# The experts' stationary operands woven: high and low words in turn, 128 bytes away from the moving weights

## The reference

```
probs / top 2 of 8 experts for each token
for an expert x:   gu = tokens_x @ w_gu[x]          # 1024 -> 2 * 2816
                   h  = silu(gu[:, :2816]) * gu[:, 2816:]
                   y  = h @ w_down[x]               # 2816 -> 1024
token = layer_norm(alpha * token + gate * y ...)
```

## Time and profile before

| what | value |
|---|---|
| median of three runs | 1770.74 us |
| the profiled execution, its own time | 1766.83 us |
| its span in the trace | 1765.0 us |
| TensorE matmul busy | 1743.4 us, 99% of the span |
| VectorE busy | 1361.9 us, 77% |
| ScalarE busy | 1076.1 us, 61% |
| granted TensorE clock, mean | 0.996 of full speed |
| DMA, mean over the span | 254 GB/s |

### The profile page before, as it was taken

The page is one execution under the profiler, slowest core; times in us unless marked ns, Lnnn a source line. Parts: engine busy times, 40 slices in busy tenths (PEclk is TensorE's granted clock), DMA queues, the critical chain, the costliest instruction groups (busy, mean ns, idle before and its releaser), DMA issues.

```text
span 1765.0 us, 26513 instructions
## 1 busy us (share of the span) xinstructions
PE 1743.4 (99%) x11249; PEld 1571.6 (89%) x11249; DVE 1361.9 (77%) x1591; ACT 1076.1 (61%) x1200; POOL 157.7 (9%) x165
## 2 busy tenths in 40 slices
PE   9999999999999999999999999999999999999997
PEld 8999999999988999998998888888888888888885
DVE  6895488677764667656687899888889898889897
ACT  7654455565644454443446777777777777767674
POOL 1454170000000100000030100000000000000110
PEclk9999999999999999999999999999999999999999
DMA  9332364656556555565463699999999999999994
GB/s 290 120 109 72 118 176 136 226 180 194 192 188 203 193 172 172 183 228 187 128 225 112 232 376 378 378 342 384 369 385 339 383 371 383 333 379 375 381 390 171
DMA packets 265206, 447.90 MB, mean 254 GB/s; under 512 B 11461, under 2 KB 135848, under 8 KB 264952
## 3 DMA queue, kind: packets, MB, share of 16 engines
q1 hardware_dynamic: 263464, 440.36, 71.5%
q0 software_dynamic: 1616, 5.77, 0.8%
HBM read 438.99 MB, written 4.73 MB: 251 GB/s over the span
## 4 chain that ended last, share of the span: by engine, by line
PE 90%; DVE 6%; ACT 3%; issue 1%; DMA 0%; SPq 0%; DVEq 0%; ACTq 0%
PE bank L428 27%; PE bank L429 27%; PE bank L430 27%; DVE ring_r L418 3%; PE bank L3240 1%; ACT hi_ring L403 1%; PE bank L3154 1%; PE bank L2522 1%; PE bank L1348 1%; PE bank L1340 1%; DVE arena L923 1%; PE bank L1832 1%; PE bank L2503 0%; PE bank L2152 0%; PE bank L1817 0%
## 5 line engine op out<-in xcount | busy, mean ns | idle before, releaser
L418 DVE TENSOR_TENSOR ring_r<-ring,hi_ring 128x2048 fp32r<-128x2048 f32 x401 | 905.4, 2285 | 260.8 <-ACT hi_ring L403 260.5
L403 ACT CAST hi_ring<-ring 128x2048 fp32r<-128x2048 f32 (+1 forms) x404 | 757.3, 1904 | 133.1 <-PE bank L430 126.7
L428 PE MATMUL bank<-hi_ring,arena_r 128*128 128x512 f32 (+1 forms) x1526 | 568.5, 373 | 2.1 <-DVE ring_r L418 2.1
L429 PE MATMUL bank<-ring_r,arena_r 128*128 128x512 f32 (+2 forms) x1534 | 566.2, 369 | 0.0
L430 PE MATMUL bank<-hi_ring,arena_r 128*128 128x512 f32 (+1 forms) x1526 | 564.3, 370 | 0.0
L428 PE MATMUL bank<-ring_r,hi_ring 128*128 128x256 f32 (+1 forms) x1400 | 397.6, 284 | 0.3 <-DVE ring_r L487 0.3
L429 PE MATMUL bank<-ring_r,hi_ring 128*128 128x256 f32 (+1 forms) x1400 | 392.8, 281 | 0.0
L430 PE MATMUL bank<-ring_r 128*128 128x256 f32 (+1 forms) x1400 | 392.7, 280 | 0.0
L428 PEld LDWEIGHTS bank<-hi_ring,arena_r 128*128 128x128 f32 x1526 | 286.6, 188 | 54.0 <-DVE ring_r L418 4.9
L429 PEld LDWEIGHTS bank<-ring_r,arena_r 128*128 128x128 f32 (+1 forms) x1534 | 287.7, 188 | 48.9
L430 PEld LDWEIGHTS bank<-hi_ring,arena_r 128*128 128x128 f32 x1526 | 286.6, 188 | 50.0
(11 more groups left out here) (436 smaller groups left out, 1571.2 us busy)
## 6 DMA issues: line engine op xcount, KB each, us to landing
ring<-in_w_gu_moe SPq DMA_DIRECT2D x176, 1024.0 KB, 7.7
ring<-in_w_down_moe SPq DMA_DIRECT2D x88, 1024.0 KB, 6.4
ring<-in_w_in SPq DMA_DIRECT2D x31, 1024.0 KB, 5.5
ring<-in_w_gu_dense SPq DMA_DIRECT2D x22, 1024.0 KB, 5.1
ring<-in_w_up SPq DMA_DIRECT2D x16, 1024.0 KB, 5.6
ring<-in_w_down SPq DMA_DIRECT2D x16, 1024.0 KB, 5.0
ring<-in_w_in_a SPq DMA_DIRECT2D x10, 1024.0 KB, 5.8
ring<-in_w_down_dense SPq DMA_DIRECT2D x10, 1024.0 KB, 5.1
```

The source lines that it names most:

```text
L403: q.e.copy(hi_ring[:, b:b + m], ring[:, a:a + m]).then_inc(*q.did(("hi", of.tag, i)))
L418: q.e.tensor_tensor(ring_r[:, a:a + m], ring[:, a:a + m], hi_ring[:, b:b + m].bitcast(F32), ALU.subtract).then_inc(*q.did(("lo", of.tag, i)))
L428: q.e.matmul(ps, a[0], b[0], start=first, stop=False)
L429: q.e.matmul(ps, a[0], b[1], start=False, stop=False)
```

## The change

A new kind of access is brought in, and `xs2` and `hp` are placed with them. `Woven` stores a pair in one region with high and low words in turn: word 2n is the high word n, word 2n + 1 the low one. A load of the stationary operand then reads 128 words with a step of two, over 1024 bytes instead of 512, and ScalarE and VectorE write high and low words with a step of two. All regions from `ST` to `hp` move down by 16 words (64 bytes). Modulo 256 bytes the stationary operands then begin 128 bytes away from the moving weights. The number of instructions, their shapes, their order and all waits stay.

```diff
+class Woven:
+    def __init__(self, a, tiles, part):
+        self.tiles, self.n = tiles, a.shape[1] // (2 * tiles)
+        self.words = a.rearrange("p (n h) -> p n h", h=2)[:, :, part]
+
+    def __getitem__(self, at):
+        _, k, cols = at
+        a, b = cols.start or 0, cols.stop or self.n
+        if isinstance(k, slice) and b - a < self.n:
+            return self.words.rearrange("p (k n) -> p k n", k=self.tiles)[:, k, a:b]
+        k0, k1 = (k.start, k.stop - 1) if isinstance(k, slice) else (k, k)
+        return self.words[:, k0 * self.n + a:k1 * self.n + b]
...
+    def woven_at(o, tiles, n):
+        a = at(o, 2 * tiles * n, of=arena_r)
+        return Pair(Woven(a, tiles, 0), Woven(a, tiles, 1))
...
-    ST = [at(9624 + 256 * j, SEQ, of=arena_r) for j in range(4)]
-    xs2 = pair_at(10648, 8, 2 * P)
-    hh, hp = at(14744, 2816), pair_at(17560, 22, P)
+    ST = [at(9608 + 256 * j, SEQ, of=arena_r) for j in range(4)]
+    xs2 = woven_at(10632, 8, 2 * P)
+    hh, hp = at(14728, 2816), woven_at(17544, 22, P)
...
-        act_split(q, flat(hp.hi[:, f:f + turned(f), :]), R.banks(R.tag, "turn", x, f)[:, 0:n], ("ps", R.tag, "turn", x, f), ("hphi", R.tag, x, f))
+        act_split(q, hp.hi[:, f:f + turned(f), :], R.banks(R.tag, "turn", x, f)[:, 0:n], ("ps", R.tag, "turn", x, f), ("hphi", R.tag, x, f))
...
-        dve_split(q, flat(hp.hi[:, f:f + turned(f), :]), flat(hp.lo[:, f:f + turned(f), :]), R.banks(R.tag, "turn", x, f)[:, 0:n], ("hphi", R.tag, x, f), ("hp", R.tag, x, f))
+        dve_split(q, hp.hi[:, f:f + turned(f), :], hp.lo[:, f:f + turned(f), :], R.banks(R.tag, "turn", x, f)[:, 0:n], ("hphi", R.tag, x, f), ("hp", R.tag, x, f))
```

## The result

The change made the kernel slower: 1777.93 us median of 5 runs (1775.01 to 1779.08) against 1768.58 us of the kernel before in the same 5 rounds (1767.08 to 1770.81). The ratio is 1.0047, with a 95% interval from 1.0032 to 1.0061. I had forecast 1744 us, with a range that reached up to 1788.

What follows compares the result with a forecast made beforehand. TensorE was taken as the bound, through the distance between matmul starts. Terms of -28.0, -2.0 and +4 us sum to -26.0 from 1766.8, so 1740.8; plus 3.9 for the median, 1744.7, given as 1744 us, range 1729 to 1788.

Steps and rivals of the forecast that it cites:

- term 1: 2976 matmuls of 512 columns in the experts' stage: distance between starts falls from 229 to 219.6 ns, -28.0 us.
- The premise of a fixed relation: Excess of 6.3, 11.6 or 15.6 ns over the columns' time comes from stream and load meeting in SBUF.
- Term 2: 384 matmuls of 256 columns: distance between starts falls from 118.3 to 113 ns, -2.0 us.
- Terms 3 and 4: ScalarE's and VectorE's writes of hp and xs2 with a step, and the transposes' operand hh moved 64 bytes: 0 each.
- Terms 5 and 6: DMA supply tight in the up part, +2 us; start and end of the experts waiting for blocks, +2 us.
- the second one: Rival: the wider load meets the stream oftener, excess doubles, +50.9 us, 1822 us; chance of slower 0.26.
- 1787: Variant of the slower rival: load walks against the stream, a third more meetings, +16.7 us.
- No change: Rival: the excess is a hand-over price independent of addresses, so 1768 to 1774 us stand; chance 0.12.

Runs made afterwards that it cites:

- e1: Step of two without the 64-byte move, against the kernel before: 512-column matmuls start 233.3 ns apart instead of 229.0, ratio 1.0073.
- e11: Step of one, xs2 and hp at 0 bytes modulo 256 from the moving weights, against the kernel before: 1765.59 us against 1770.87, ratio 0.9976.
- e3: First map: kernel before, step of one, each expert's hp and each pair's xs2 at another place: 227.2 to 234.3 ns between starts.
- e9: Map of e3 with the moving weights 64 bytes higher, stationary operands unmoved: 227.2 ns at 0 bytes, 229.0 at 192, 232.3 at 128.
- e10: Kernel before with 512 down to 256 columns moved, by expert: excess over the columns' time 15.6 ns at 512, 10.8 at 256.
- e5: Kernel before with fewer columns loaded, by expert: starts 229.1 ns apart with 128 columns, 233.3 with 96, 228.3 with 64, 231.2 to 232.1 with 32.
- e13: Map of e3 with only 32 of 128 columns loaded; together with a map of the remaining places, 228.4 to 239.0 ns between starts.
- e6: Map of e3 with a step of four words: loads take 313 ns instead of 188, whole kernel 1841.0 us (one run).

## Why the prediction was wrong

- **What bounds the kernel** was right: TensorE, by the distance between starts. It gives 12.8 of the 13.05 us of e1 and 8.4 of the 9.35 us of the change. (The sum's 1744.7 rounds to 1745, not to 1744; nothing rests on it.)
- **The step that failed is term 1**, the price of 219.6 ns for two reads of one speed. It measured 231.5, so +7.4 us and not -28.0 us. The argument had two parts, and both fell. First, that reads of nearly one speed stay apart: step two, at 19 distances over the whole 256 bytes, is never below 230.1 ns. Second, that 6.3 ns is what reads cost that hardly meet. I took it from 256-column matmuls, of another stage and with other operands, and gave it to 512-column ones. The price doesn't carry over: at 0 bytes (e11) 256-column matmuls are at their dearest with a step of one, 119.7 ns (below, 15 distances in 1.80 us), an excess of 13.0, while 512-column ones are at their cheapest, an excess of 13.8. The lowest excess that any of the full loads showed at 512 columns is 13.8 ns (227.1), so of the 15.6 ns that I wanted to win back, 1.8 were to be had, and not by weaving.

```profile
1425.64 0.28 PE L429 MATMUL bank<-ring_r,arena_r 128*128 128x256 f32 x1
...
1427.44 0.28 PE L429 MATMUL bank<-ring_r,arena_r 128*128 128x256 f32 x1
```

- **The premise of a fixed relation** was the deeper fault. From three numbers (6.3, 11.6, 15.6 ns) I concluded that the excess grows with the stream and depends on meetings. Of this, the dependence on place is shown (e3, e9); the growth is weak (e10), and the proportion to the load's reads is wrong (e5, e13).
- **Term 2**: 384 matmuls of 256 columns went from a mean of 116.7 to 120.7 ns, +1.5 us instead of -2.0. Before, experts 0 and 2 were at 113.3 ns already, and the others at 117.8.
- **Terms 3 and 4** were right at 0. VectorE's writes took 685 instead of 682 ns; ScalarE's 45 ns more, covered as said.
- **Terms 5 and 6** never came into play, since TensorE got slower; the DMAs moved 365 instead of 370 GB/s.
- **The rivals.** The measured time lies on the side of the second one, but its mechanism isn't what happened either: the load visits twice the memory at every distance, and yet step two is slower than step one at 192 bytes (+4.3 ns), faster at 64 (-3.1) and at 128 (-0.8 to -1.4). The "1787" had a size from speeds that add, which nothing bears out. "No change" has the time nearly right (1768 to 1774 us against 1777.93), but the interval of the ratio excludes it, and its reason is wrong: addresses do count. None of my cases held "other place of an uneven map", which is what it was: 229.0 to 231.5, within the 7 ns that places differ by.
- **What stays open** is why the map is as it is: which accesses of a load disturb which of the stream, why the same place can settle in two patterns, and what the 13.8 ns that no place removes are. That the two reads affect each other is shown by the places, but that they do so by meeting is argued only. The walk direction of the load wasn't tried.

## What to carry to other kernels

If TensorE starts float32r matmuls back to back, the distance between starts in the timeline is the number to watch, and where operands lie relative to each other modulo 256 bytes was worth up to 7 ns of 229 on each of them here; a map with another place for each repeated piece of work finds it in one run, and no argument found it here. A layout change with a rearranged operand always changes two things, the pattern and the place, so try each alone ahead of any theory on the pair. And before a price is taken from a similar instruction, look whether the two move together: at 0 bytes 256-column matmuls cost most and 512-column ones least.

## What the runs showed of the hardware

- A load with a step of two float32r words is on record for 195 to 196 ns instead of 188, with a step of four for 313. A load takes 0.82 ns a word (188, 162, 134, 109 ns for 128, 96, 64, 32).
- Code that isn't touched takes different times from one execution to the next, in steps: the 7601st matmul of the program, just ahead of the experts, starts 986.7 us into the span at the earliest and 993.7 at the latest among the 15 kernels (those before and after among them) in which all that lies ahead of the experts and the moving weights are as before; the earlier trace rows and the 873 and 863 matmuls above show how, a run of 256-column matmuls keeps to 113 or to 118 ns once it is in either. That is nearly as large as the effect of this change, and of the size by which 15 runs of the kernel before spread, from 1765.36 to 1772.43 us.
- ScalarE writes with a step of two words 45 ns slower per 512 words (634 against 589 ns), VectorE doesn't (685 against 682). With a step of four both do: 1101 ns for ScalarE and 1123 for VectorE (e6).
- With a step of one and 128 columns loaded, 256-column matmuls stand at 113.3 or 117.8 ns at 192 bytes and at 119.7 at 0.
